# Two float32r products of a rounded sum and its difference in place of one fp32 product, for twelve means of squares

## The chip, the core and the metric

The kernel runs on one core of one Trainium2 chip. The metric is the device time of one execution in microseconds (us), the median over runs. Its engines work side by side, each through its own list of instructions in order, and wait for each other at semaphores: PE (TensorE, matrix products), ACT (ScalarE), DVE (VectorE), POOL (GpSimd) and SP (SyncE, which here issues the DMAs).

## The reference

A trunk of four layers over x of shape 1 x 512 x 1024. Each layer adds a token mixer and then a feed-forward layer to the residual stream, and each of the two starts with a root-mean-square norm:

```python
def _rmsnorm(x, g):
    xf = x.astype(jnp.float32)
    y = xf * lax.rsqrt(jnp.mean(xf * xf, axis=-1, keepdims=True) + EPS)
    return (y * g.astype(jnp.float32)).astype(x.dtype)

def _conv_ffn(h, w_up, conv_w, conv_b, w_down):
    u = _causal_dwconv(h @ w_up, conv_w, conv_b)
    return (jax.nn.silu(u[..., D_FF:]) * u[..., :D_FF]) @ w_down

for i in range(DEPTH):
    hn = _rmsnorm(x, mix_norm[i])
    ...
    x = x + mix.astype(x.dtype)
    x = x + _conv_ffn(_rmsnorm(x, ffn_norm[i]), ffn_w_up[i], ffn_conv_w[i], ffn_conv_b[i],
                      ffn_w_down[i]).astype(x.dtype)
```

The mixers are an RG-LRU block, a Mamba-2 SSD, sliding-window attention and HGRN2, in this order. HGRN2 has 8 heads, and normalises the output `o` of each head by itself, over its 128 features:

```python
    o = _rmsnorm(o, norm_w).reshape(bsz, s, D_MODEL) * jax.nn.silu(g_out.astype(jnp.float32))
```

## The kernel before

Everything is stored with features on the 128 partitions and the 512 tokens along the free dimension. x is 8 tiles of 128 x 512 (`k.x`). Weights come in panels of 128 x 1024 words by DMA into a ring of 4 (`k.w`). ACT rounds a panel to float32r (`round_until`, L250, into `w_big`), and POOL subtracts that from the panel and writes the difference as bf16 (`weights_gpsimd`, L266, four pieces of 128 x 256, into `w_rest`). A tile of a product with weights is then 8 float32r products (`in_big`, L295) and 8 bf16 products (`in_rest`, L305), summed in one PSUM bank; output products do the same at L337 and L341. POOL passes the panels strictly in order, in one loop over all panels at the end of the program.

A norm over features is a product with a constant 128 x 128 matrix `mean` of 1/1024: it sums over partitions and leaves the mean in every row. The squares are made by ACT (`square_x`, L399) and summed over the 8 tiles by DVE (`sum_squares`, L475, the last into `sqsum`). `norm_tensor` (L585) is the product, in fp32. ACT then takes the logarithm and the exponential (`inverse_root`, L553 and L556) for `rstd`, by which DVE scales what the projection left in PSUM (L693 in the feed-forward layer). The projection itself doesn't wait for the norm. In the feed-forward layer (`ffn_tensor`) `norm_tensor` stands inside panel 1, between its float32r and its bf16 products. ACT rounds panels 4 and 5 only after its first work on panels 0 and 1 (`ffn_scalar`), which needs `rstd`.

In the HGRN2 mixer `hgrn_events` writes out the order of all engines by hand. A slot holds half a panel of the projection ("half": 4 products L295, 4 products L305), one of 8 levels of the attention of an earlier head (L1833 to L1848, with DVE's updates L2018, L2019, L2021 and L2032 between two levels), and the steps of a "tail" of a still earlier head. A head takes 8 slots and 4 panels. Tail step 3 is the output of the head (L1879, L1882) and ACT's square of it (L1929, into `k.sq`); step 4, one slot later, is the mean (L1887, an fp32 product) and ACT's logarithm and exponential into `inner_factor`; steps 6 to 8 finish the head: DVE L2053, L2058, ACT L1937, DVE L2061, and after the last head PE needs L2061's output for the last products of the output projection (L337, L341). For the last two heads the slots have no projection left, and pieces of the output projection ("early") take its place.

## Time and profile before

| | |
|---|---|
| time, median of 3 runs | 1772.92 us (1772.85 to 1773.04) |
| the profiled execution's own time | 1772.94 us |
| its span in the trace | 1771.1 us |
| PE busy | 1720.5 us, 97% of the span |
| DVE, ACT, POOL busy | 1150.9, 1129.3, 1227.8 us |
| granted TensorE clock | 9 tenths or more in all 40 slices |

The span runs from the first instruction of the trace to the end of the last; 1.8 us of the execution's time lie outside it. Busy time of an engine counts a stretch in which several of its instructions overlap once. A record of a matrix product starts when it is issued and ends when its last column is out, so records in a row overlap, and it is the distance of two starts that says what a product costs. PEld is the loading of the weights of a product, which lies beside the products before it.

### The profile page before, as it was taken

Reading aid. Unit: us, or ns where it says so; the run is one execution under the profiler, and the core shown is the slowest. Engines: PE = TensorE matmul, PEld = TensorE weight load, DVE = VectorE, ACT = ScalarE, POOL = GpSimd, SP = SyncE. Lnnn points to the kernel's source line nnn. Section 1 sums busy time; section 2 is a strip of 40 time slices with the busy share of each in tenths; the row PEclk is TensorE's granted clock in tenths of the full one; section 3 lists DMA queues with packets and bytes.
Section 4 is the critical chain, followed back from the end, with each engine's and each line's share of the span. In section 5 each row is a group of like instructions: output and inputs, shape, how many; then the busy total and the mean of one; then the engine's idle time right before and its main releaser. Section 6 shows DMA issues by size and latency. Waiting matters only on the chain.

```text
span 1771.1 us, 27487 instructions
## 1 busy us (share of the span) xinstructions
PE 1720.5 (97%) x9861; PEld 1040.6 (59%) x10032; DVE 1150.9 (65%) x1873; ACT 1129.3 (64%) x1581; POOL 1227.8 (69%) x1788
## 2 busy tenths in 40 slices
PE   7989999999999999999999999999999999999999
PEld 4546666655555556666665666666655565566665
DVE  6886777228888754777226857776248877577720
ACT  8887666455977757666555877665454555866642
POOL 7747777877555647777877657778865554677785
PEclk9999999999999999999999999999999999999999
DMA  7323444545223225444543114444532222344453
GB/s 270 107 96 120 152 145 148 154 154 158 74 95 104 86 82 175 147 144 149 153 149 108 37 38 150 152 143 147 154 128 97 97 96 73 108 154 145 152 153 122
DMA packets 65615, 226.59 MB, mean 128 GB/s; under 512 B 8149, under 2 KB 9173, under 8 KB 64981
## 3 DMA queue, kind: packets, MB, share of 16 engines
q1 hardware_dynamic: 64236, 221.88, 39.6%
q10 hardware_dynamic: 1245, 2.95, 0.5%
q8 instruction: 80, 1.31, 0.3%
q14 instruction: 54, 0.44, 0.1%
HBM read 222.51 MB, written 2.10 MB: 127 GB/s over the span
## 4 chain that ended last, share of the span: by engine, by line
PE 73%; DVE 10%; ACT 8%; issue 5%; POOL 3%; DMA 1%; ACTq 0%; DVEq 0%; POOLq 0%
PE psum L295 22%; PE psum L305 21%; PE psum L337 12%; PE psum L341 11%; POOL w_rest L266 2%; ACT w_big L250 2%; DMA y_rest<-in_ssd_tables 1%; DVE psum L1621 1%; PE psum L1833 1%; PE psum L2241 1%; ACT psum L1468 1%; PE psum L2276 1%; DVE psum L1706 1%; PE psum L2258 1%; ACT L1501 1%
## 5 line engine op out<-in xcount | busy, mean ns | idle before, releaser
L266 POOL TENSOR_TENSOR w_rest<-w_panel,w_big 128x256 bf16<-128x256 f32 x1660 | 1163.9, 740 | 461.1 <-ACT w_big L250 461.1
L295 PE MATMUL psum<-x_big,w_big 128*128 128x512 f32 x2248 | 656.1, 425 | 8.5 <-ACT x_big L387 6.4
L305 PE MATMUL psum<-x_rest,w_rest 128*128 128x512 bf16 x2131 | 537.7, 382 | 8.7 <-DVE x_rest L483 1.7
L250 ACT ACTIVATE w_big<-w_panel 128x1024 fp32r<-128x1024 f32 (+1 forms) x415 | 418.4, 1032 | 171.9 <-PE psum L341 91.4
L295 PEld LDWEIGHTS psum<-x_big,w_big 128*128 128x128 f32 x2248 | 416.3, 189 | 134.7 <-issue 25.8
L305 PEld LDWEIGHTS psum<-x_rest,w_rest 128*128 128x128 bf16 x2248 | 188.6, 98 | 283.2 <-issue 102.6
L701 DVE SCALAR_TENSOR_TENSOR psum<-ffn_raw,params,psum 128x512 f32<-128x512 f32 x352 | 264.6, 752 | 7.2 <-ACT psum L655 1.0
L693 DVE TENSOR_TENSOR ffn_raw<-psum,rstd 128x512 f32<-128x512 f32 x176 | 121.4, 691 | 138.9 <-PE psum L305 120.3
L655 ACT ACTIVATE psum<-ffn_raw,params 128x512 f32<-128x512 f32 x176 | 137.4, 782 | 102.1 <-DVE ffn_raw L693 101.8
L337 PE MATMUL psum<-g_big,w_big 128*128 128x512 f32 x704 | 199.4, 423 | 0.0
L547 DVE SCALAR_TENSOR_TENSOR x_resid<-psum,x_resid 128x512 f32<-128x512 f32 x64 | 43.8, 689 | 225.0 <-PE psum L341 202.2
L341 PE MATMUL psum<-g_rest,w_rest 128*128 128x512 bf16 x677 | 165.4, 381 | 1.3
L337 PEld LDWEIGHTS psum<-g_big,w_big 128*128 128x128 f32 x704 | 133.2, 189 | 36.0
L662 ACT ACTIVATE g_big<-psum 128x512 fp32r<-128x512 f32 x88 | 52.5, 597 | 111.2 <-DVE psum L710 111.1
L341 PEld LDWEIGHTS psum<-g_rest,w_rest 128*128 128x128 bf16 x704 | 61.1, 98 | 87.8 <-issue 26.5
L337 PE MATMUL psum<-y_big,w_big 128*128 128x512 f32 x320 | 107.8, 459 | 2.1 <-DVE y_rest L2061 1.1
L483 DVE SCALAR_TENSOR_TENSOR x_rest<-x_big,psum 128x512 bf16<-128x512 f32 x64 | 43.9, 686 | 90.7 <-ACT psum L391 90.7
L341 PE MATMUL psum<-y_rest,w_rest 128*128 128x512 bf16 x298 | 84.1, 383 | 2.5 <-POOL w_rest L266 1.8
L337 PEld LDWEIGHTS psum<-y_big,w_big 128*128 128x128 f32 x320 | 60.3, 191 | 18.8 <-issue 5.2
L710 DVE TENSOR_TENSOR psum<-psum,ffn_silu_out 128x512 f32<-128x512 f32 x88 | 61.5, 699 | 7.0 <-ACT ffn_silu_out L678 4.1
L387 ACT ACTIVATE x_big<-x_resid,shifted_gain 128x512 fp32r<-128x512 f32 x64 | 45.4, 710 | 31.6 <-DVE x_resid L547 31.6
L714 DVE SCALAR_TENSOR_TENSOR g_rest<-g_big,psum 128x512 bf16<-128x512 f32 x88 | 59.8, 680 | 2.7 <-ACT g_big L662 2.7
(263 smaller groups left out, 1714.1 us busy)
## 6 DMA issues: line engine op xcount, KB each, us to landing
w_panel<-in_up SPq DMA_DIRECT2D x176, 512.0 KB, 3.5
w_panel<-in_dn SPq DMA_DIRECT2D x64, 448.0 KB, 3.3
w_panel<-in_ssd_in SPq DMA_DIRECT2D x41, 512.0 KB, 3.2
w_panel<-in_dn SPq DMA_DIRECT2D x32, 512.0 KB, 3.5
w_panel<-in_hgrn_in SPq DMA_DIRECT2D x32, 512.0 KB, 3.2
w_panel<-in_lru_in SPq DMA_DIRECT2D x18, 512.0 KB, 3.5
w_panel<-in_ssd_out SPq DMA_DIRECT2D x16, 512.0 KB, 3.2
w_panel<-in_swa_in SPq DMA_DIRECT2D x12, 512.0 KB, 3.2
```

What stands on the lines that cost most here:

```text
L250: act.activation(k.w1[:, slot, 0:words], k.w[:, slot, 0:words], ACT.Copy, scale=(SHIFT - 1) / SHIFT).then_inc(k.s("panel_big"), 1)
L266: rest = pool.tensor_tensor(k.w2[:, slot, a], k.w[:, slot, a], k.w1[:, slot, a].bitcast(F32), ALU.subtract)
L295: pe.matmul(out, k.w1[:, slot, q * m:(q + 1) * m], k.x1[:, q, :], start=q == 0, stop=False)
L305: mm = pe.matmul(out, k.w2[:, slot, q * m:(q + 1) * m], k.x2[:, q, :], start=False, stop=q == DT - 1)
L337: pe.matmul(out, k.w1[:, slot, (q - p0) * P:(q - p0 + 1) * P], y1[:, q, :], start=q == 0, stop=False)
L341: mm = pe.matmul(out, k.w2[:, slot, (q - p0) * P:(q - p0 + 1) * P], y2[:, q, :], start=False, stop=q == kt - 1)
L655: act.activation(out, k.ffn_raw[:, j % 2, half, 2:], ACT.Identity, bias=k.p("ffn_conv_b", j + (l * 2 * FF_T + half * FF_T)), scale=k.p("ff ...
L662: act.activation(k.g1[:, j, :], k.ps[:, lin_bank(j), :], ACT.Copy, scale=1 / SHIFT).then_inc(k.s("ffn_hi"), 1)
L693: dve.tensor_tensor(k.ffn_raw[:, j % 2, half, 2:], k.ps[:, k.bank(job, i), :], k.rstd[:, :], ALU.mult).then_inc(k.s("banks_free"), 1)
L701: dve.scalar_tensor_tensor(out, k.ffn_raw[:, j % 2, half, tap:tap + S], k.p("ffn_conv_w", j + ((l * 3 + tap) * 2 * FF_T + half * FF_T)), o ...
L710: dve.tensor_tensor(out, out, k.ffn_silu[:, j % 2, :], ALU.mult).then_inc(k.s("ffn_gated"), 1)
L714: dve.scalar_tensor_tensor(k.g2[:, j, :], k.g1[:, j, :].bitcast(F32), 1 - SHIFT, k.ps[:, lin_bank(j), :], ALU.mult, ALU.add).then_inc(k.s( ...
```

## The change

Twelve of the mean products change: the four of the feed-forward layers and the eight of HGRN2's heads. The other norms keep theirs. Instead of one fp32 product of `mean` with the squares there are two products in float32r: one with the squares rounded to float32r, one with what the rounding left, also float32r, added in the same PSUM bank.

In the feed-forward layer DVE makes the two parts from `sqsum` (`part_squares`: a copy that rounds, and a subtraction), and PE's two products move behind the bf16 products of panel 1 (`norm_in_parts`). In HGRN2 ACT squares the head's output twice, once in fp32 and once rounded (`x_sq_high`), and POOL subtracts (`hgrn_gpsimd`), at a place in its loop over the panels: before the weights of panel 4h + 11 for head h, and before panel 36 for the last. PE has the product with the rounded part first and the one with the rest behind it, each with its own wait. `mean` is rounded once to float32r at the start, by DVE. The new tiles lie over `x_sq` and `x_sqsum`; `mean_big` is new (512 bytes of each partition). The last piece is a semaphore: the SSD mixer's `ssd_ea` is now counted in `ssd_decays`.

```diff
+        self.sq_parts = sb("x_sq_parts", [P, 2, S], F32R)
+        self.sq_high = sb("x_sq_high", [P, S], F32R)
...
+        self.mean = sb("mean_big", [P, P], F32R)
...
+def part_squares(dve, k, c):
+
+    dve.wait_ge(k.s("sq_summed"), (DT - 1) * (c + 1))
+    dve.tensor_copy(k.sq_parts[:, 0, :], k.sqsum[:, :]).then_inc(k.s("sq_parted"), 1)
+    dve.wait_ge(k.s("sq_parted"), c + (HG_H if c == 2 * DEPTH - 1 else 0))
+    dve.tensor_tensor(k.sq_parts[:, 1, :], k.sqsum[:, :], k.sq_parts[:, 0, :].bitcast(F32), ALU.subtract
+                      ).then_inc(k.s("sq_parted"), 1)
...
             dve.wait_ge(k.s("params_landed"), 32)
+            dve.tensor_copy(k.mean[:, :], k.c("mean"))
             shift_gain(dve, k, 2, DEPTH - 1)
...
+        if c % 2:
+            part_squares(dve, k, c)
...
+def norm_in_parts(pe, k, l):
+
+    parted = 2 * l + (HG_H if l == DEPTH - 1 else 0)
+    pe.wait_ge(k.s("sq_parted"), parted + 1)
+    pe.matmul(k.ps[:, 4, :], k.mean[:, :], k.sq_parts[:, 0, :], start=True, stop=False)
+    pe.wait_ge(k.s("sq_parted"), parted + 2)
+    pe.matmul(k.ps[:, 4, :], k.mean[:, :], k.sq_parts[:, 1, :], start=False, stop=True
               ).then_inc(k.s("norm_summed"), 1)
...
-        if i == 1:
-            norm_tensor(pe, k, 2 * l + 1)
         pe.wait_ge(k.s("panel_split"), k.split(job, i))
         in_rest(pe, k, job, i, fresh=None if i else 2 * l + 1)
+        if i == 1:
+            norm_in_parts(pe, k, l)
...
-            pe.wait_ge(k.s("hgrn_sq"), h + 1)
-            pe.matmul(k.ps[:, 4, :], k.c("mean"), k.sq[:, h % 2, :], start=True, stop=True
+            pe.wait_ge(k.s("hgrn_sq"), 2 * h + 2)
+            pe.matmul(k.ps[:, 4, :], k.mean[:, :], k.sq_high[:, :], start=True, stop=False)
+            pe.wait_ge(k.s("sq_parted"), 2 * DEPTH - 2 + h + 1)
+            pe.matmul(k.ps[:, 4, :], k.mean[:, :], k.sq_parts[:, h % 2, :], start=False, stop=True
                       ).then_inc(k.s("hgrn_sum"), 1)
...
-            act.activation(k.sq[:, h % 2, :], k.ps[:, 7, :], ACT.Square, scale=mean_scale(P)).then_inc(k.s("hgrn_sq"), 1)
+            if h:
+                act.wait_ge(k.s("hgrn_sum"), h)
+            for out in (k.sq[:, h % 2, :], k.sq_high[:, :]):
+                act.activation(out, k.ps[:, 7, :], ACT.Square, scale=mean_scale(P)).then_inc(k.s("hgrn_sq"), 1)
...
+def hgrn_gpsimd(pool, k, panel):
+
+    for h in range(HG_H):
+        if panel == min(4 * h + 11, 4 * HG_H + 4):
+            pool.wait_ge(k.s("hgrn_sq"), 2 * h + 2)
+            sq = k.sq[:, h % 2, :]
+            pool.tensor_tensor(k.sq_parts[:, h % 2, :], sq, k.sq_high[:, :].bitcast(F32), ALU.subtract
+                               ).then_inc(k.s("sq_parted"), 1)
...
             for n in range(FIRST, len(PANELS)):
                 ssd_gpsimd(pool, k, n - k.panel0["ssd_in"])
+                hgrn_gpsimd(pool, k, n - k.panel0["hgrn_in"])
                 weights_gpsimd(pool, k, n)
```

Three places of the order of instructions, of before and then of the change. The numbers of lines are those of each kernel: L295, L305, L1833, L1887 and L266 of before are L301, L311, L1861, L1915 with L1917, and L272 of the change. First PE, around the mean of one head in HGRN2, before:

```order
L295 MATMUL psum<-x_big,w_big 128x512 x4
L305 MATMUL psum<-x_rest,w_rest 128x512 [waits panel_split]
L305 MATMUL psum<-x_rest,w_rest 128x512 x3
L1833 MATMUL psum<-arena 32x16 [waits hgrn_attn,hgrn_update]
L1833 MATMUL psum<-arena 32x16 x15
L1887 MATMUL psum<-x_sq,consts 128x512 [waits hgrn_sq]
L295 MATMUL psum<-x_big,w_big 128x512 [waits banks_free,panel_big]
```

The same place of the change:

```order
L301 MATMUL psum<-x_big,w_big 128x512 x4
L311 MATMUL psum<-x_rest,w_rest 128x512 [waits panel_split]
L311 MATMUL psum<-x_rest,w_rest 128x512 x3
L1861 MATMUL psum<-arena 32x16 [waits hgrn_attn,hgrn_update]
L1861 MATMUL psum<-arena 32x16 x15
L1915 MATMUL psum<-x_sq_high,mean_big 128x512 [waits hgrn_sq]
L1917 MATMUL psum<-x_sq_parts,mean_big 128x512 [waits sq_parted]
L301 MATMUL psum<-x_big,w_big 128x512 [waits banks_free,panel_big]
```

Nothing moved; the second product has a wait of its own, on POOL, and the next half of a panel stands behind it. Next POOL in the change, the stretch that has the subtractions of the last two heads (of before it is L266 throughout):

```order
L272 TENSOR_TENSOR w_rest<-w_panel,w_big 128x256 [waits panel_big]
L272 TENSOR_TENSOR w_rest<-w_panel,w_big 128x256 x3
L1984 TENSOR_TENSOR x_sq_parts<-x_sq,x_sq_high 128x512 [waits hgrn_sq]
L272 TENSOR_TENSOR w_rest<-w_panel,w_big 128x256 [waits panel_big]
L272 TENSOR_TENSOR w_rest<-w_panel,w_big 128x256 x3
L1984 TENSOR_TENSOR x_sq_parts<-x_sq,x_sq_high 128x512 [waits hgrn_sq]
L272 TENSOR_TENSOR w_rest<-w_panel,w_big 128x256 [waits panel_big]
```

For each head the subtraction stands behind the four pieces of panel 4h + 10 and ahead of those of panel 4h + 11; that of the last head follows the panel behind its predecessor's. Last PE in a feed-forward layer, panel 1, before:

```order
L295 MATMUL psum<-x_big,w_big 128x512 x7
L585 MATMUL psum<-x_sqsum,consts 128x512 [waits sq_summed]
L305 MATMUL psum<-x_rest,w_rest 128x512 [waits panel_split]
L305 MATMUL psum<-x_rest,w_rest 128x512 x7
L295 MATMUL psum<-x_big,w_big 128x512 [waits banks_free,panel_big]
```

The same place of the change:

```order
L301 MATMUL psum<-x_big,w_big 128x512 x7
L311 MATMUL psum<-x_rest,w_rest 128x512 [waits panel_split]
L311 MATMUL psum<-x_rest,w_rest 128x512 x7
L611 MATMUL psum<-x_sq_parts,mean_big 128x512 [waits sq_parted]
L613 MATMUL psum<-x_sq_parts,mean_big 128x512 [waits sq_parted]
L301 MATMUL psum<-x_big,w_big 128x512 [waits banks_free,panel_big]
```

The mean moved behind the 8 bf16 products of panel 1.

## Rows read from the trace of the kernel before

**Rows 1.** The page: its chain of waits by engine; PE's busy time.

```profile
PE 73%; DVE 10%; ACT 8%; issue 5%; POOL 3%; DMA 1%; ACTq 0%; DVEq 0%; POOLq 0%
...
PE 1720.5 (97%) x9861; PEld 1040.6 (59%) x10032; DVE 1150.9 (65%) x1873; ACT 1129.3 (64%) x1581; POOL 1227.8 (69%) x1788
```

**Rows 2.** Stretch of one HGRN2 head: length, busy us (count) by engine, clock, DMA.

```profile
1394.59:1417.85 23.26, 22.83 (x316) 14.06 (x319) 18.81 (x43) 12.51 (x16) 12.06 (x17) 1.00 0.29 92
```

**Rows 3.** Timeline, PE, last feed-forward layer: start, length, engine, line, tiles, count, idle before.

```profile
1531.60 0.50 PE L295 MATMUL psum<-x_big,w_big 128*128 128x512 f32 x1 [0.18 <-ACT x_big L387]
1531.94 1.90 PE L305 MATMUL psum<-x_rest,w_rest 128*128 128x512 bf16 x8
1533.49 2.21 PE L295 MATMUL psum<-x_big,w_big 128*128 128x512 f32 x8
1535.54 1.02 PE L585 MATMUL psum<-x_sqsum,consts 128*128 128x512 f32 x2
...
1537.94 2.17 PE L295 MATMUL psum<-x_big,w_big 128*128 128x512 f32 x8
1539.95 1.90 PE L305 MATMUL psum<-x_rest,w_rest 128*128 128x512 bf16 x8
1541.50 2.19 PE L295 MATMUL psum<-x_big,w_big 128*128 128x512 f32 x8
...
1547.11 1.25 PE L305 MATMUL psum<-x_rest,w_rest 128*128 128x512 bf16 x5
```

**Rows 4.** Timeline of the same stretch, DVE, ACT and POOL.

```profile
1533.63 0.69 DVE L475 TENSOR_TENSOR x_sqsum<-x_sq,psum 128x512 f32<-128x512 f32 x1
1536.60 0.69 ACT L553 ACTIVATE rstd<-psum,params 128x512 f32<-128x512 f32 x1 [0.20 <-PE psum L585]
1542.59 2.81 POOL L266 TENSOR_TENSOR w_rest<-w_panel,w_big 128x256 bf16<-128x256 f32 x4 [2.79 <-ACT w_big L250]
```

**Rows 5.** Timeline, one HGRN2 head (the third): ACT, PE, POOL, DVE.

```profile
1395.78 0.60 ACT L1929 ACTIVATE x_sq<-psum 128x512 f32<-128x512 f32 x1 [0.32 <-PE psum L1882]
1397.86 1.13 PE L1887 MATMUL psum<-x_sq,consts 128*128 128x512 f32 x2
1394.59 2.80 POOL L266 TENSOR_TENSOR w_rest<-w_panel,w_big 128x256 bf16<-128x256 f32 x4 [6.82 <-ACT w_big L250]
1398.73 1.01 DVE L2019 TENSOR_TENSOR arena<-arena 128x256 f32<-128x256 f32 x1
1401.54 0.41 DVE L2019 TENSOR_TENSOR arena<-arena 128x256 f32<-128x256 f32 x1
```

**Rows 6.** Timeline in the SSD mixer: POOL on 128 x 512, and PE behind it.

```profile
474.15 1.28 POOL L1548 TENSOR_TENSOR x_sqsum<-x_sqsum,x_sq 128x512 f32<-128x512 f32 x1 [1.83 <-ACT x_sq L1508]
475.48 0.30 PEld L1380 LDWEIGHTS psum<-x_sqsum,consts 128*128 128x128 f32 x2 [0.62 <-POOL x_sqsum L1548]
```

**Rows 7.** Timeline, HGRN2, seventh head: POOL and PE.

```profile
1487.64 2.79 POOL L266 TENSOR_TENSOR w_rest<-w_panel,w_big 128x256 bf16<-128x256 f32 x4 [6.84 <-ACT w_big L250]
1490.01 1.13 PE L1887 MATMUL psum<-x_sq,consts 128*128 128x512 f32 x2
1492.32 0.45 PE L1833 MATMUL psum<-arena 128*32 128x16 f32 x32 [0.28 <-DVE arena L2021]
```

**Rows 8.** Timeline, HGRN2, last head: ACT, then PE in the output projection.

```profile
1504.07 0.60 ACT L1929 ACTIVATE x_sq<-psum 128x512 f32<-128x512 f32 x1 [4.00 <-PE psum L1882]
1505.98 0.69 ACT L553 ACTIVATE inner_factor<-psum,params 128x512 f32<-128x512 f32 x1
1511.54 0.50 PE L337 MATMUL psum<-y_big,w_big 128*128 128x512 f32 x1 [1.11 <-DVE y_rest L2061]
```

**Rows 9.** Timeline, PE near the program's start.

```profile
19.87 0.60 PE L305 MATMUL psum<-x_rest,w_rest 128*128 128x512 bf16 x2 [0.78 <-DVE x_rest L483]
```

**Rows 10.** Groups by line and shape: copies of DVE and POOL; busy us, mean ns.

```profile
L1695 DVE COPY x_sqsum<-x_sq 128x512 f32<-128x512 f32 x1 | 0.4, 417 | 0.0
L1546 POOL COPY x_sqsum<-x_sq 128x512 f32<-128x512 f32 x3 | 1.8, 610 | 10.9 <-ACT x_sq L1508 10.9
```

More of the change, by code:

```diff
@@ L150, in __init__ @@
         self.factor = sb("inner_factor", [P, S])
+        at = self._at
         self.sq = sb("x_sq", [P, 2, S])
         self.sqsum = sb("x_sqsum", [P, S])
+        after, self._at = self._at, at
+        self.sq_parts = sb("x_sq_parts", [P, 2, S], F32R)
+        self.sq_high = sb("x_sq_high", [P, S], F32R)
+        self._at = after
         self.par = sb("params", [P, NPARAM])
@@ L585, in norm_tensor @@
     pe.matmul(k.ps[:, 4, :], k.c("mean"), k.sqsum[:, :], start=True, stop=True
+              ).then_inc(k.s("norm_summed"), 1)
+def norm_in_parts(pe, k, l):
[4 more added lines that the diff above has]
+    pe.matmul(k.ps[:, 4, :], k.mean[:, :], k.sq_parts[:, 1, :], start=False, stop=True
               ).then_inc(k.s("norm_summed"), 1)
@@ L1293, in turn @@
             if g == 0:
-                pe.wait_ge(k.s("ssd_decays"), 2)
+                pe.wait_ge(k.s("ssd_decays"), 3)
                 pe.wait_ge(k.s("ssd_dt_t"), 3)
@@ L1449, in dt @@
             return
-        act.activation(b.ea, k.p("ssd_a_log"), ACT.Exp).then_inc(k.s("ssd_ea"), 1)
+        act.activation(b.ea, k.p("ssd_a_log"), ACT.Exp).then_inc(k.s("ssd_decays"), 1)
         act.wait_ge(k.s("banks_free"), k.evicted("ssd_in", 0))
@@ L1576, in dt @@
             softplus_join(dve, softplus, b.size, b.q, b.dt)
-            dve.wait_ge(k.s("ssd_ea"), 1)
+            dve.wait_ge(k.s("ssd_decays"), 1)
             dve.wait_ge(k.s("ssd_ones"), 16)
@@ L1588, in decays @@
         if part == 2:
-            dve.wait_ge(k.s("ssd_decays"), 2)
+            dve.wait_ge(k.s("ssd_decays"), 3)
             dve.tensor_tensor(b.dt_end.rearrange("p c h -> p (c h)"), k.ps[:, 5, P:2 * P],
```

## The prediction

> **What bounds the kernel now.** I read the page first, then the stretches of HGRN2 and the timelines around the twelve products. The chain that ended last is PE for 73% and PE is busy for 97% of the span [rows 1]. In the middle of HGRN2 a head takes 23.26 us, of which PE is busy 22.83, while DVE has 18.81, ACT 12.51 and POOL 12.06 [rows 2]; the clock is 1.00, the 2.4 GHz level, throughout. So a product less on PE is time won, and a wait of PE is time lost at once, since its list is in order. What is left to ask at each of the twelve places is whether both parts are there when PE comes.
>
> **The product itself.** In the feed-forward layer panel 1, with the mean inside, runs from 1533.49 to 1537.94, 4.45 us; panel 2, without it, from 1537.94 to 1541.50, 3.56 [rows 3]. The fp32 product costs 0.89 us. It stands in the trace as two records (x2). Sixteen products in 3.56 us are 0.22 each; the float32r half alone, 8 from 1537.94 to 1539.95, gives 0.25 at most. I take 0.235 for one float32r product, 0.47 for the pair: 0.42 less on PE where nothing waits, bounds 0.39 and 0.45.
>
> The Trainium skill (Perfetto Trace Analysis, Engine Utilization) halves TensorE's output rate for what it calls FP32_LOW_HIGH. Taken for a whole fp32 product that would be 0.43 us, as much as the new pair, and the sum would lose its whole gain; the row has 0.89 for it, so here the halving holds for each of the two records. The measurement decides.
>
> **Feed-forward layers, four times.** DVE's last sum ends at 1533.63 + 0.69 = 1534.32 [rows 4]. The rounding copy is 0.42 as the nearest row [rows 10], the subtraction has the shape of L475, 0.69: both are done by 1535.5, or about 1536.5 if POOL, which works at this time, holds each up by half a microsecond. PE comes to the pair only after panel 1's bf16 products, at 1533.49 + 3.56 = 1537.05. No wait there. Cost of these two on DVE: nothing, DVE waits for `rstd` afterwards.
>
> But the norm is later. The second product starts at 1537.28 and lasts 0.4 (2.17 us for eight that start 0.25 apart [rows 3]), so the pair ends at about 1537.7 where the fp32 product ended at 1536.56 (1535.54 + 1.02), so ACT's logarithm moves from 1536.60 [rows 4] to about 1537.75, by 1.15 us, and with it the scaling, ACT's rounding of panels 4 and 5, and POOL's differences. POOL finishes panel 4 at 1542.59 + 2.81 = 1545.40; that becomes 1546.55, and 1546.60 at PE. PE wants panel 4's bf16 products at 1547.11 [rows 3] less 0.42 = 1546.69. It fits by 0.1 us; I charge nothing, with 0.2 each as the upper bound. Term: 4 x -0.42 = -1.7 (bounds -1.8 and -0.9).
>
> **HGRN2, heads 0 to 5.** The place is the same in all six, as in [rows 5]. ACT's square ends at 1396.38; the second one, again 0.60, at about 1397.0. PE comes to the first product at 1397.86: no wait. POOL is the question. It starts on panel 4h + 10 at 1394.59 and ends its four pieces at 1397.39; the subtraction stands behind them. POOL on two fp32 inputs of 128 x 512 takes 1.28 us, and PE's weight load starts 0.05 us behind it (475.43 to 475.48) [rows 6]. So the rest is there at 1397.39 + 1.28 + 0.05 = 1398.72, 0.86 us after PE came, and 0.6 after it has finished the first product. Behind a wait a float32r product takes 0.34 until the next one starts (1531.60 to 1531.94) [rows 3], since its weights aren't loaded ahead. PE goes on at 1399.06; before it was 1397.86 + 0.89 = 1398.75. A head costs 0.31 us more instead of 0.42 less: 6 x 0.31 = +1.9. What is queued behind the waiting product is the next half of a panel, then the next level of the attention, for which DVE waits; there it is all later by the same 0.3. POOL's next panel is 1.28 later, but PE needs it three panels on. Bounds: a POOL instruction of that shape cannot be much under the copy, 0.61 [rows 10], which would give no wait (1398.05) and -0.42 a head; and if DVE keeps it off by half a microsecond, as each holds the other up below, +0.8 a head.
>
> That they do hold each other up is in [rows 5]: DVE's L2019 on 128 x 256 takes 1.01 us at 1398.73, while POOL runs, and 0.41 at 1401.54, when POOL has stopped. The subtraction starts in a stretch in which DVE is idle, so I take the undisturbed 1.28.
>
> The Trainium skill (SBUF — State Buffer, Who interferes with whom) says that a DVE instruction with two SBUF inputs and a GpSimd instruction that reads SBUF exclude each other for a whole instruction, and whichever starts first wins. By the rows just named it holds here. It speaks against this change, as POOL's work in HGRN2 grows by 1.28 us a head, and is the second rival below.
>
> **Head 6.** Here the slots are shorter. POOL is done with its four pieces at 1487.64 + 2.79 = 1490.43 [rows 7], the rest reaches PE at 1490.43 + 1.28 + 0.05 = 1491.76, PE goes on at 1492.10 instead of 1490.01 + 0.89 = 1490.90: +1.2. Before, PE then waited for DVE until 1492.32 with 0.28 idle, which gives some of it back; but POOL's panel 35 now also runs 1.28 later into DVE's next level, which takes some again. Term: +1.1, bounds 0.7 and 1.6.
>
> **Head 7.** POOL is free, and the chain is short of everything: in the output projection PE waits 1.11 us for this head's L2061 at 1511.54 [rows 8]. So each added step counts in full. The square ends at 1504.67; the second square adds 0.60 (1505.27), POOL 0.05 + 1.28 (1506.60), PE's second product starts at 1506.65 and ends 0.50 later (the record at 1531.60 [rows 3]), and with the same small distance the logarithm starts at about 1507.2 instead of 1505.98: +1.25, bounds 1.1 and 1.6. PE's filler in between gets 1.4 later and still ends before.
>
> **The start.** DVE's copy of `mean` stands ahead of a sum and of an `x_rest` for which PE waits for 0.78 us [rows 9]. A copy of 128 x 512 takes 0.42 [rows 10], a quarter of it with the fixed part perhaps 0.15: +0.15 (0 to 0.3).
>
> **Nothing else.** The semaphore renamed in the SSD mixer is waited for at the same places. ACT's eight squares in heads 0 to 6 and POOL's 1.28 us a head lie on engines half idle [rows 2]. No DMA is moved.
>
> **Sum**, against the profiled execution's own time of 1772.94: -1.7 + 1.9 + 1.1 + 1.25 + 0.15 = +2.7, so 1775.6; the median of the runs shown is 0.02 lower, which changes nothing. With every term at its lower bound it would be -1.8 - 2.5 + 0.7 + 1.1 + 0 = -2.5 (1770.4), with every term at its upper -0.9 + 4.8 + 1.6 + 1.6 + 0.3 = +7.4 (1780.3); all at once is unlikely at either end. A measurement of this kernel can tell 0.2%, 3.5 us, from no change: below 1769.4 is faster, above 1776.4 slower. The forecast is within, on the slow side.
>
> **The rivals.**
> 1. *PE waits for POOL* (the forecast): 1775.6. Chance 0.53.
> 2. *POOL and DVE hold each other up* (slower). POOL's subtraction and the panel behind it fall into DVE's updates of the next levels; DVE's L2021 ends later than PE comes to the level, in each of the six heads, or DVE holds the subtraction itself up. If it is 0.5 us a head for six heads and 0.4 in the last two: +2.7 + 3.4 = +6.1, 1779. For it: L2019's 1.01 us. Against it: DVE idles long before this place and PE's own delay gives it 0.3 us. It decides if more than about 0.3 us of DVE's delay isn't covered by PE's. Chance 0.2.
> 3. *Both parts are there in time* (the other side). All twelve pairs save 0.42: -5.0 + 0.15, 1768.1, faster. It needs the rest at PE by 1398.1, a subtraction in under 0.7 us or POOL starting earlier. For it: POOL's copy of that size takes 0.61. Against: L1548 with the same operands takes 1.28, and even at 0.65 the last head's chain has grown by the second square and the subtraction. Chance 0.1.
> 4. *The pair costs what the fp32 product did*, that is the change doesn't do what it says: the feed-forward term is 0 and HGRN2's heads get the second product's half more, 8 x 0.2: +2.7 + 1.7 + 1.6 = +6.0, 1778.9. Against: 0.25 at most for a float32r product in rows 3. Chance 0.05.
> The remaining 0.12 is for what I don't see, spread to both sides.
>
> **How the numbers follow.** Predicted is the first case, 1775.6. The range is 1771.0 to 1779.0: its lower end leaves out rival 3 and half of the unseen, its upper end takes in most of rival 2. Slower: rivals 2 and 4 (0.24), a fifth of the forecast whose terms are all near their upper bounds (0.11), and part of the unseen: 0.38. Faster: rival 3 and a little: 0.12. Within 0.2%: 0.50.
>
> **What would show it.** In the profile after: PE's second product of heads 0 to 5 waits about 0.6 us for POOL's L1984, which starts when its four pieces end and takes 1.28; a head takes 23.57 us instead of 23.26; the last head's `inner_factor` starts 3.1 us after the start of the first square instead of 1.9; in the feed-forward layers the second product ends 1.1 us later in its panel than the fp32 one and PE doesn't wait at panel 4. It is wrong if L1984 takes well under or over 1.28, if PE waits at DVE's L2021 more than before, or if PE's gain in the feed-forward layers isn't 0.42 each.

## The result, and the profile after

The change takes 1775.55 us (median of 20 runs, 1774.9 to 1776.6) where the kernel before takes 1772.84 (20 runs beside them, 1772.2 to 1773.15): +2.7 us, ratio 1.0016, 95% interval 1.0009 to 1.0023. That is slower, by less than the 0.2% that the prediction called no change. The profiled execution spans 1773.6 us (before 1771.1). Of all executions in this document two are left out of every median and comparison, one of the kernel before (9918 us) and one of experiment 7 (2470 us, at a granted clock of 0.655).

The page, its chain by engine and its busy times, which answer to [rows 1]:

```profile
PE 1718.4 (97%) x9861; PEld 1039.2 (59%) x10032; DVE 1164.5 (66%) x1882; ACT 1132.5 (64%) x1589; POOL 1242.3 (70%) x1796
...
PE 72%; DVE 10%; ACT 8%; issue 5%; POOL 4%; DMA 1%; ACTq 0%; DVEq 0%; POOLq 0%
```

PE works 2.1 us less and the span is 2.5 us longer, so PE waits 4.6 us more. The waits of PE that are new or have grown most, from the list of waits (us in total, times, longest):

```profile
PE psum L1917 <- POOL x_sq_parts L1984: 4.0, 8, 1.2
...
PE psum L1915 <- ACT x_sq_high L1962: 1.2, 1, 1.2
```

The first is the wait of the second product of each of the eight heads for POOL's subtraction. The second is the last head's wait for the second square, where the kernel before waited 0.7 us for its one square; 4.0 and 0.5 are nearly all of the 4.6.

**Heads 0 to 5.** The stretch of one head, with the same columns as [rows 2]:

```profile
1393.94:1417.48 23.54, 22.78 (x315) 14.06 (x319) 19.57 (x43) 12.90 (x17) 13.64 (x17) 1.00 0.28 91
```

A head takes 23.54 us instead of 23.26, PE is busy 0.05 less, DVE 0.76 more in the same 43 instructions, POOL 1.58 more. From one head's square to the next it is 23.52 to 23.55 in all six. The third head in the timeline, as [rows 5] before:

```profile
1397.26 0.50 PE L1915 MATMUL psum<-x_sq_high,mean_big 128*128 128x512 f32 x1
1398.09 0.50 PE L1917 MATMUL psum<-x_sq_parts,mean_big 128*128 128x512 f32 x1 [0.32 <-POOL x_sq_parts L1984]
1398.42 1.09 PE L301 MATMUL psum<-x_big,w_big 128*128 128x512 f32 x4
1399.36 1.04 PE L311 MATMUL psum<-x_rest,w_rest 128*128 128x512 bf16 x4
1400.32 0.45 PE L1861 MATMUL psum<-arena 128*32 128x16 f32 x32
...
1405.18 0.64 PE L1876 MATMUL psum<-arena 128*32 128x64 f32 x16
...
1395.19 0.60 ACT L1962 ACTIVATE x_sq<-psum 128x512 f32<-128x512 f32 x1 [0.32 <-PE psum L1910]
1395.68 0.59 ACT L1962 ACTIVATE x_sq_high<-psum 128x512 fp32r<-128x512 f32 x1
...
1393.99 2.80 POOL L272 TENSOR_TENSOR w_rest<-w_panel,w_big 128x256 bf16<-128x256 f32 x4 [6.85 <-ACT w_big L256]
1396.76 1.27 POOL L1984 TENSOR_TENSOR x_sq_parts<-x_sq,x_sq_high 128x512 fp32r<-128x512 f32 x1
1397.99 3.17 POOL L272 TENSOR_TENSOR w_rest<-w_panel,w_big 128x256 bf16<-128x256 f32 x4
1402.50 3.21 POOL L272 TENSOR_TENSOR w_rest<-w_panel,w_big 128x256 bf16<-128x256 f32 x4 [1.34 <-ACT w_big L256]
...
1398.93 0.95 DVE L2064 TENSOR_TENSOR arena<-arena 128x256 f32<-128x256 f32 x1
...
1403.28 0.97 DVE L2062 TENSOR_TENSOR arena<-arena 128x256 f32<-128x256 f32 x1
1404.18 0.94 DVE L2064 TENSOR_TENSOR arena<-arena 128x256 f32<-128x256 f32 x1
```

POOL's L1984 stands right behind its four pieces, takes 1.27 us and ends at 1398.03; PE's second product starts at 1398.09 and the half panel behind it 0.33 later. That is the wait that was forecast. Two details matter below. DVE's L2064 (L2021 of before) ends at 1399.88, and the next level, which needs it, starts at 1400.32, so PE's own delay leaves DVE 0.44 us here. Two levels later L2064 ends at 1405.12 and PE's L1876 starts at 1405.18: there PE comes no sooner than DVE lets it.

**The last two heads.** PE, ACT, with [rows 7, 8] for before:

```profile
1492.22 0.50 PE L1917 MATMUL psum<-x_sq_parts,mean_big 128*128 128x512 f32 x1 [1.20 <-POOL x_sq_parts L1984]
...
1508.15 0.50 PE L1917 MATMUL psum<-x_sq_parts,mean_big 128*128 128x512 f32 x1 [0.85 <-POOL x_sq_parts L1984]
...
1514.24 0.50 PE L343 MATMUL psum<-y_big,w_big 128*128 128x512 f32 x1 [1.00 <-DVE y_rest L2104]
...
1505.67 0.60 ACT L1962 ACTIVATE x_sq<-psum 128x512 f32<-128x512 f32 x1 [4.00 <-PE psum L1910]
...
1508.68 0.69 ACT L571 ACTIVATE inner_factor<-psum,params 128x512 f32<-128x512 f32 x1 [0.63 <-PE psum L1917]
```

From the seventh head's square to the last one's it is 16.33 us instead of 15.24 (+1.09). In the last head `inner_factor` starts 3.01 us after the square instead of 1.91 (+1.10).

**The feed-forward layers.** The last one, PE, ACT and DVE, as [rows 3, 4] before:

```profile
1536.19 2.19 PE L301 MATMUL psum<-x_big,w_big 128*128 128x512 f32 x8
...
1539.78 0.58 PE L611 MATMUL psum<-x_sq_parts,mean_big 128*128 128x512 f32 x1
1540.20 0.39 PE L613 MATMUL psum<-x_sq_parts,mean_big 128*128 128x512 f32 x1
1540.43 2.02 PE L301 MATMUL psum<-x_big,w_big 128*128 128x512 f32 x8
...
1547.43 2.19 PE L301 MATMUL psum<-x_big,w_big 128*128 128x512 f32 x8
...
1551.06 2.20 PE L301 MATMUL psum<-x_big,w_big 128*128 128x512 f32 x8
...
1540.63 0.69 ACT L571 ACTIVATE rstd<-psum,params 128x512 f32<-128x512 f32 x1 [1.53 <-PE psum L613]
...
1536.33 0.69 DVE L481 TENSOR_TENSOR x_sqsum<-x_sq,psum 128x512 f32<-128x512 f32 x1
1537.05 0.90 DVE L488 CAST x_sq_parts<-x_sqsum 128x512 fp32r<-128x512 f32 x1
1537.98 1.11 DVE L490 TENSOR_TENSOR x_sq_parts<-x_sqsum,x_sq_parts 128x512 fp32r<-128x512 f32 x1
```

PE waits for neither part. Panel 1 with the pair takes 4.24 us (1536.19 to 1540.43) instead of 4.45, and the panel behind it gives back another 0.17. From the first weight load of panel 1 to that of panel 3 it is 7.61 to 7.66 us in the four layers, before 8.00 to 8.04: -0.40 each. Then the panel with tile 4 takes 3.63 instead of 3.58, and a few hundredths follow; at panel 8 the layers stand at -0.28 to -0.31, so 0.1 us each is given back.

### The profile page after: what moved, and what is told of

Its sections match the earlier page's. It is cut to its first block, busy times and chain, and to the rows that moved or that the text cites. A ratio compares the mean times of both kernels' runs of the same rounds, so it can differ in the third digit from the quotient of the medians.

```text
span 1773.6 us, 27519 instructions
## 1 busy us (share of the span) xinstructions
PE 1718.4 (97%) x9861; PEld 1039.2 (59%) x10032; DVE 1164.5 (66%) x1882; ACT 1132.5 (64%) x1589; POOL 1242.3 (70%) x1796
## 4 chain that ended last, share of the span: by engine, by line
PE 72%; DVE 10%; ACT 8%; issue 5%; POOL 4%; DMA 1%; ACTq 0%; DVEq 0%; POOLq 0%
PE psum L301 22%; PE psum L311 21%; PE psum L343 12%; PE psum L347 11%; POOL w_rest L272 3%; ACT w_big L256 2%; DMA y_rest<-in_ssd_tables 1%; DVE psum L1649 1%; PE psum L2284 1%; ACT psum L1496 1%; PE psum L1861 1%; PE psum L2319 1%; DVE psum L1734 1%; POOL x_sq_parts L1984 1%; PE psum L2301 1%
## 5 line engine op out<-in xcount | busy, mean ns | idle before, releaser
L272 POOL TENSOR_TENSOR w_rest<-w_panel,w_big 128x256 bf16<-128x256 f32 x1660 | 1168.8, 742 | 437.8 <-ACT w_big L256 437.8
L301 PE MATMUL psum<-x_big,w_big 128*128 128x512 f32 x2248 | 652.3, 423 | 8.7 <-ACT x_big L393 6.6
L311 PE MATMUL psum<-x_rest,w_rest 128*128 128x512 bf16 x2131 | 537.1, 381 | 8.8 <-DVE x_rest L498 1.9
L301 PEld LDWEIGHTS psum<-x_big,w_big 128*128 128x128 f32 x2248 | 415.7, 189 | 132.8 <-issue 23.6
L311 PEld LDWEIGHTS psum<-x_rest,w_rest 128*128 128x128 bf16 x2248 | 188.3, 98 | 282.0 <-issue 101.1
```

The lines of the kernel that those rows point to most:

```text
L272: rest = pool.tensor_tensor(k.w2[:, slot, a], k.w[:, slot, a], k.w1[:, slot, a].bitcast(F32), ALU.subtract)
L301: pe.matmul(out, k.w1[:, slot, q * m:(q + 1) * m], k.x1[:, q, :], start=q == 0, stop=False)
L311: mm = pe.matmul(out, k.w2[:, slot, q * m:(q + 1) * m], k.x2[:, q, :], start=False, stop=q == DT - 1)
```

## The experiments

Times in one table, each beside the kernel before on the same chip (1772.84 for the change, 1772.93 to 1772.99 for the experiments). "Head" is the distance between the squares of two neighbouring heads among the first seven, in the profiled execution. An interval that holds 1, as in 1, 8 and 11, doesn't tell the time from that of the kernel before by itself; what these three are used for is read from their traces. The eleven executions of 1 (1771.13 to 1772.34 us) and the 28 of the kernel before beside them (1772.34 to 1773.72) meet only at their ends all the same.

| | us | ratio to before, 95% | head |
|---|---|---|---|
| before | 1772.9 | | 23.26 |
| the change | 1775.55 | 1.0009 to 1.0023 | 23.53 |
| 1: feed-forward part alone | 1771.76 | 0.9985 to 1.0002 | 23.25 |
| 2: HGRN2 part alone | 1777.35 | 1.0016 to 1.0035 | 23.54 |
| 3: subtraction one panel earlier | 1777.74 | 1.0016 to 1.0036 | 23.5 to 23.6 |
| 4: PE's pair one slot later | 1776.19 | 1.0011 to 1.0028 | 23.58 |
| 5: one product, nothing subtracted | 1771.33 | 0.9981 to 0.9998 | 22.62 |
| 6: DVE subtracts | 1771.09 | 0.9981 to 0.9999 | 22.88 to 22.99 |
| 7: as 5, POOL has less to do | 1768.58 | 0.9965 to 0.9984 | 22.62 |
| 8: as 1, pair inside panel 1 | 1771.72 | 0.9985 to 1.0002 | 23.26 |
| 9: as 6, last head in fp32 | 1770.53 | 0.9978 to 0.9995 | 22.88 to 22.97 |
| 10: the change, POOL has less to do | 1775.30 | 1.0003 to 1.0022 | 23.43 |
| 11: 4 and 10 together | 1772.95 | 0.9991 to 1.0009 | 23.02 |

**1 and 2, the two halves of the change.** In 1 HGRN2's squares, product and place in POOL's loop are those of before, in 2 `norm_tensor` of the feed-forward layers is.

```diff
-                hgrn_gpsimd(pool, k, n - k.panel0["hgrn_in"])
```

> HGRN2's heads go back to the fp32 product without POOL's subtraction and ACT's second square; the feed-forward layers keep the pair. Theory (PE saves 0.4 us per pair where the parts are ready, and loses in HGRN2 by waiting for POOL): 0.15 us more at the start, 0.3 less in each feed-forward layer, so 1 us below the kernel before, about 1771.8. Rival (the pair is no cheaper than one fp32 product, all of the change's difference is in products): same as before or up to 0.9 us (a third of the change's +2.7) above it.

```diff
-        if c % 2:
-            part_squares(dve, k, c)
...
-        if i == 1:
-            norm_in_parts(pe, k, l)
+        if i == 1:
+            norm_tensor(pe, k, 2 * l + 1)
```

> The feed-forward layers go back to the fp32 product in its old place; HGRN2 keeps the pair, POOL's subtraction and the second square. Theory: 0.15 at the start, 6 heads x 0.27, head 6 1.1 and head 7 1.1 more: +3.95, about 1776.8, slower than the change as a whole. Rival (the loss is spread over all twelve places): about +1.8, 1774.6.

Measured 1771.76 and 1777.35: -1.2 and +4.4, together +3.2 where the change has +2.7. Both halves do what their terms say, the first as a gain, the second as a loss. Heads take 23.25 us in 1, as before, and 23.54 in 2, as in the change. In the profile of 2 the first head's square is already 0.6 us late (1349.84 against 1349.27 before), though nothing but the copy of `mean` is added ahead of it; in the change it is 1.1 early, of which three feed-forward layers make 0.9. What stands ahead of HGRN2 varies by some tenths from trace to trace, and that is as much as the 0.5 by which the halves don't add up.

**3, the subtraction one panel earlier in POOL's loop**, ahead of panel 4h + 10 instead of 4h + 11, so that it is done before PE comes.

```diff
-        if panel == min(4 * h + 11, 4 * HG_H + 4):
+        if panel == min(4 * h + 10, 4 * HG_H + 4):
```

> POOL's subtraction of heads 0 to 6 stands one panel earlier, before panel 4h+10. Theory: in heads 0 to 5 POOL waits for the second square and subtracts at once, PE's wait falls from about 0.6 to 0.1 us, a head costs 0.3 less than before instead of 0.25 more: -1.8 for six heads; heads 6 and 7 as in the change (+2.2), feed-forward -1.2, start +0.15: -0.65, about 1772.2. Rival (POOL and DVE hold each other up, it is the added POOL work that costs): POOL's two panels end 3 us later and fall wholly into DVE's updates of the next levels, so no gain or a loss against the change: 1775.5 or more.

Measured 1777.74: the theory that PE's wait is the whole matter failed. In heads 0 to 5 PE's second product doesn't wait for POOL any more (in head 6 it still does, for 0.81 us), yet those heads keep their 23.5 to 23.6 us. In the third head the level behind the pair starts 4.72 us after the square, 0.22 sooner than before the change, and the head still ends 0.28 later than then, so the loss lies behind that slot. POOL now waits for the head's square before it may touch panel 4h + 10, and then works without a pause beside DVE's updates. Its timeline, and the wait of PE that grew, from the list of waits (in the change that row has 2.3 us):

```profile
1349.81 1.27 POOL L1984 TENSOR_TENSOR x_sq_parts<-x_sq,x_sq_high 128x512 fp32r<-128x512 f32 x1 [9.71 <-ACT x_sq_high L1962]
1351.04 13.67 POOL L272 TENSOR_TENSOR w_rest<-w_panel,w_big 128x256 bf16<-128x256 f32 x16
```

```profile
PE psum L1907 <- DVE arena L2091: 4.9, 8, 1.5
```

More than half of what 3 has above the change comes behind the seventh head: from its square to the last one's it is 17.59 us instead of 16.33. There POOL works on two panels for 6.59 us without a pause, and PE waits for DVE's L2064 before three levels, 0.43, 0.97 and 0.92 us.

**4, PE's pair one slot later** in heads 0 to 6, behind the next level and 2.3 us after L1984 is done.

```diff
-        elif t == 4:
+        elif t == (4 if h == HG_H - 1 else 5):
```

> PE's pair of heads 0 to 6 stands one slot later (about 2.8 us of PE's other work later); POOL, ACT and DVE do what they do in the change. Theory (it is PE's wait that costs): no wait at POOL's L1984 in heads 0 to 6, each of heads 0 to 5 costs 0.4 less than before, head 6 about nothing, head 7 still +1.1, feed-forward -1.2, start +0.15: -2.4, about 1770.4. Rival (contention of POOL with DVE costs, and PE would wait for DVE's updates anyway): the heads keep their 23.5 us, about 1775.5.

Measured 1776.19, heads 23.58: no gain, and the theory failed again, as in 3. The third head:

```profile
1399.64 0.44 PE L1861 MATMUL psum<-arena 128*32 128x16 f32 x32 [0.59 <-DVE arena L2064]
1400.01 0.50 PE L1915 MATMUL psum<-x_sq_high,mean_big 128*128 128x512 f32 x1
1400.35 0.39 PE L1917 MATMUL psum<-x_sq_parts,mean_big 128*128 128x512 f32 x1
...
1398.64 0.94 DVE L2064 TENSOR_TENSOR arena<-arena 128x256 f32<-128x256 f32 x1
```

The pair no longer waits, and in its place the level waits for DVE's L2064, which ran beside POOL and took 0.94. PE then still has the pair before it, 0.56 us (1400.01 to 1400.57). The profiled execution of 4 took as long as the change's (1775.56 and 1775.45 us). Its median is 0.6 higher, and part of that is the clock: its executions at a mean granted clock of 1.000 took 1775.63 to 1776.12 us, those at 0.999 up to 1777.11, and the profiled one has the granted clock at 0.50 for some 3.3 us in the last head.

**5 and 7, one product of the rounded squares.** 5 leaves out the second square, POOL's subtraction and the second product, so the mean is that of the rounded squares; 7 also leaves out three of POOL's four pieces of panels 4h + 11, so that part of the weights' differences isn't computed.

```diff
-            for out in (k.sq[:, h % 2, :], k.sq_high[:, :]):
-                act.activation(out, k.ps[:, 7, :], ACT.Square, scale=mean_scale(P)).then_inc(k.s("hgrn_sq"), 1)
+            act.activation(k.sq_high[:, :], k.ps[:, 7, :], ACT.Square, scale=mean_scale(P)).then_inc(k.s("hgrn_sq"), 1)
...
-                hgrn_gpsimd(pool, k, n - k.panel0["hgrn_in"])
```

> HGRN2's heads have one float32r product alone, of the rounded squares (the rest that the rounding leaves is left out of the mean), no subtraction on POOL and no second square; the feed-forward layers keep the pair (alone 1771.8). PE's product is 0.65 us shorter than the fp32 one and nothing is waited for. Theory of the prediction (in heads 0 to 5 PE's own work is the bound): 8 x -0.65 = -5.2, about 1766.6. Theory after the last runs (in the slot of the mean the next level waits for DVE's three updates, which POOL's panel holds up by 1.5 us, and the fp32 product only fills that time): a head gains 0.1 to 0.2 us, the last 0.4: about 1770.6.

```diff
+    short = 11 <= at_hgrn < 4 * HG_H and at_hgrn % 4 == 3
-    for at in range(0, words, PIECE):
+    for at in range(3 * PIECE if short else 0, words, PIECE):
```

> As e5_one_product, and POOL leaves out three of the four pieces of each panel 4h+11 of HGRN2's input (those products use what the ring held before), so that it isn't at work during DVE's updates in the slot of the mean. Theory of the prediction: as e5 without it, 1766.6, whatever POOL does. Theory after the last runs: DVE's L2062 and L2064 fall from 1.0 and 0.95 to 0.41 there, the level no longer waits, and the whole 0.65 a head comes: 3 us or more below e5, about 1767.

Measured 1771.33 and 1768.58. Both profiles show heads of 22.62, 0.64 less than before. But the profiled execution of 5 took 1768.39 us, and the other ten took 1770.56 to 1771.98, so that its profile is not that of a typical run; 7 has no such gap (1767.49 profiled, the others 1768.1 to 1769.3). With less for POOL to do, the median falls by 2.75 us. Where the typical run of 5 loses them isn't on record: no trace of one was taken. Two of DVE's updates in the slot of the mean, beside POOL in 5, and the second of them alone in 7:

```profile
1396.24 0.19 DVE L2058 TENSOR_TENSOR arena<-arena 128x32 f32<-128x32 f32 x1 [2.93 <-PE psum L1861]
...
1397.24 0.95 DVE L2061 TENSOR_TENSOR arena<-arena 128x256 f32<-128x256 f32 x1
```

```profile
1395.83 0.42 DVE L2063 TENSOR_TENSOR arena<-arena 128x256 f32<-128x256 f32 x1
```

The profiled execution of 5 shows one thing more. The small update L2058, the first of the slot, took 0.19 us there; at the same place it took 0.67 in the change and 0.80 before. So DVE was done 4.17 us after the square, where in the change it was 4.69, and PE, which came at 4.31, didn't wait. With the 0.67 of the change DVE would be done at about 4.65 and each head be some 0.35 us longer, which in seven heads is 2.4 us, near the 2.9 between this execution and the median of 5. That is an estimate from these rows, and no trace of a typical execution shows it.

**10 and 11, whether PE's wait costs anything.** Experiments 3 and 4 took PE's wait away and gained nothing. Either that wait is harmless, or each of the two put something in its place. 10 is the change with POOL's three pieces left out, 11 has the later pair of 4 as well; that part of the weights' differences isn't computed in either.

```diff
+    short = 11 <= at_hgrn < 4 * HG_H and at_hgrn % 4 == 3
-    for at in range(0, words, PIECE):
+    for at in range(3 * PIECE if short else 0, words, PIECE):
```

> The change itself, but POOL leaves out three of the four pieces of panels 4h + 11, the ones behind its subtraction; that part of the weights' differences is not computed. POOL is then away from DVE's updates of the next levels (PE's wait for the subtraction stays as it is). Theory 'two limits' (PE's wait for POOL and DVE's updates beside POOL are each enough to keep a head near 23.5): heads 0 to 5 take 23.3 to 23.5 us, the time is 1774 to 1775.5 us. Rival 'DVE's updates alone': heads at 22.9, 1771 us.

```diff
-        elif t == 4:
+        elif t == (4 if h == HG_H - 1 else 5):
```

> Both limits taken away at once: PE's pair one slot later in heads 0 to 6, and POOL leaves out three of the four pieces of panels 4h + 11; that part of the weights' differences is not computed. Theory 'two limits': heads 0 to 5 fall to 22.85 us (0.41 under the kernel before), the time is 1770.5 us (1769.5 to 1771.5), where each of the two alone stays at 1774 or more. Rival (something third holds the heads at 23.5): 1775 us or more.

| length of a head, us | POOL as in the change | POOL has less to do |
|---|---|---|
| pair in its place | 23.53 | 23.43 |
| pair one slot later | 23.58 | 23.02 |

With the pair in its place POOL's work matters little (0.10); with the pair one slot later it decides (0.56). The third head's rows show why: the level behind the pair, and DVE's update that it needs. 10, then 11:

```profile
1398.65 0.50 PE L1919 MATMUL psum<-x_sq_parts,mean_big 128*128 128x512 f32 x1 [0.33 <-POOL x_sq_parts L1986]
...
1400.88 0.30 PE L1863 MATMUL psum<-arena 128*32 128x16 f32 x13
...
1399.50 0.41 DVE L2066 TENSOR_TENSOR arena<-arena 128x256 f32<-128x256 f32 x1
```

```profile
1398.51 0.45 PE L1863 MATMUL psum<-arena 128*32 128x16 f32 x32
...
1398.05 0.41 DVE L2066 TENSOR_TENSOR arena<-arena 128x256 f32<-128x256 f32 x1
```

In 10 DVE is done at 1399.91, and PE, held by the subtraction, comes 0.97 later. In 11 DVE is done at 1398.46 and PE starts at 1398.51. The same for all kernels of interest, counted from the start of the third head's (first) square, to about 0.01 us:

| us after the square | DVE's update done | level starts | pair, or fp32 product | next level starts |
|---|---|---|---|---|
| before | 4.82 | 4.94 | ahead | 7.32 |
| the change | 4.69 | 5.13 | ahead, with a wait | 7.52 |
| 4 | 4.68 | 4.73 | behind | 7.57 |
| 10 | 4.17 | 5.13 | ahead, with a wait | 7.51 |
| 11 | 4.16 | 4.21 | behind | 7.05 |
| 6 | 4.61 | 4.66 | ahead, no wait | 7.06 |
| 5, as profiled | 4.17 | 4.31 | ahead, one product | 6.68 |

Beside POOL, DVE's update is a floor for the level: the level can't start before it. It lies at 4.6 to 4.8 in the four rows in which POOL is beside all of DVE's updates (before, the change, 4 and 6) and at 4.2 in 10 and 11; only the profiled execution of 5 has 4.2 with POOL there. What PE does ahead of the level costs nothing up to there. In the change the wait lifts PE over the floor, by 0.44. In 4 PE reaches the floor early, idles, and then pays the pair behind it in full: the wait is gone and so is the cover. In 11 the floor itself is 0.5 lower. So PE's wait is the cause in its slot, and moving the pair was no cure.

Of 11's time the 1770.5 that was expected failed, by 2.4. The six heads took 23.02 instead of 22.85, which is 1.0 us. In the seventh the level now waits 1.67 us for DVE, in 4 and in 11 alike, in place of the change's wait for POOL; so 4 has 16.31 us from the seventh square to the last, no less than the change's 16.33, where "about nothing" above the 15.24 of before was expected. In 11 that stretch is even 17.22, and there it is the clock. PE in 11 behind the wait, and the stretch from that level to the start of L1890, which follows two levels later; then the same stretch in 4, from 1493.22 to L1888 (the columns are those of [rows 2]):

```profile
1490.40 0.45 PE L1863 MATMUL psum<-arena 128*32 128x16 f32 x32 [1.67 <-DVE arena L2066]
...
1490.40:1496.89 6.49, 6.49 (x78) 3.64 (x79) 4.66 (x13) 2.60 (x3) 2.18 (x3) 0.74 0.35 126
```

```profile
1493.22:1498.80 5.58, 5.08 (x79) 2.92 (x79) 4.68 (x13) 2.60 (x3) 2.18 (x3) 1.00 0.33 106
```

The granted clock was at 1.00 during the wait, fell to its lower level of 1.2 GHz about 0.7 us behind it and was back at about 1494.3 (mean 0.51 between). That made the stretch 0.91 us longer than in 4, where the clock stayed at 1.00 behind the same wait; why it fell in one and not in the other is open. Eight of 11's ten executions have a mean granted clock of 0.999 and took 1772.74 to 1773.90 us, the two at 1.000 took 1772.04 and 1772.34. For the profiled executions, 6 x 0.51 less and 0.9 more is -2.2 against the change; their times differ by 2.1 (1773.36 and 1775.45).

**6 and 9, DVE subtracts.** DVE idles when the second square is done. In 6 it takes the subtraction from POOL in all eight heads; in 9 the last head goes back to one square and the fp32 product, since its chain has nothing to hide the pair's steps. 9 contains the edit of 6.

```diff
-                hgrn_gpsimd(pool, k, n - k.panel0["hgrn_in"])
...
+        if t == 3:
+            dve.wait_ge(k.s("hgrn_sq"), 2 * h + 2)
+            dve.tensor_tensor(k.sq_parts[:, h % 2, :], k.sq[:, h % 2, :], k.sq_high[:, :].bitcast(F32), ALU.subtract
+                              ).then_inc(k.s("sq_parted"), 1)
```

> The change with its subtraction in HGRN2 on DVE, in the 2.9 us in which DVE idles before the slot of the mean, and nothing of it on POOL; the pair, both squares and the feed-forward layers as in the change. Theory (POOL's extra 1.28 us delays PE's second product and pushes POOL's panel further over DVE's updates): heads 0 to 5 are at or up to 0.2 us below their 23.26 before, head 6 about as before, head 7 +0.6 (second square, 0.69 for 1.28): 1771.8 with the feed-forward layers' gain, 3.8 below the change. Rival (any second product and second square costs what the change does): 1775.5.

```diff
+            if h == HG_H - 1:
+                pe.wait_ge(k.s("hgrn_sq"), 2 * h + 1)
+                pe.matmul(k.ps[:, 4, :], k.c("mean"), k.sq[:, h % 2, :], start=True, stop=True
+                          ).then_inc(k.s("hgrn_sum"), 1)
+                return
```

> The version in which DVE subtracts, and the last head keeps the fp32 product with one square. The last head's chain then has no second square (0.49 us) and no subtraction (0.69) but an fp32 product for two float32r ones (0.42 more): 0.6 to 0.8 us less than with the pair. Theory: heads 0 to 5 stay at 22.9 us, the time is 1770.4 us against 1771.1 with the pair in all eight heads and 1772.9 before. Rival (the last head's chain is covered by PE's other work there): 1771.1 again.

Measured 1771.09 and 1770.53. Both beat the kernel before; 9 is the fastest version that computes everything, 2.4 us under before and 5.0 under the change. The third head in 6, DVE and PE:

```profile
1395.66 1.05 DVE L2086 TENSOR_TENSOR x_sq_parts<-x_sq,x_sq_high 128x512 fp32r<-128x512 f32 x1 [1.83 <-ACT x_sq_high L1962]
...
1398.20 0.94 DVE L2064 TENSOR_TENSOR arena<-arena 128x256 f32<-128x256 f32 x1
```

```profile
1396.62 0.50 PE L1915 MATMUL psum<-x_sq_high,mean_big 128*128 128x512 f32 x1
1396.96 0.39 PE L1917 MATMUL psum<-x_sq_parts,mean_big 128*128 128x512 f32 x1
...
1399.20 0.45 PE L1861 MATMUL psum<-arena 128*32 128x16 f32 x32
```

The rest is there at 1396.71, and both products run without a wait. The level starts at 1399.20, 0.06 behind the end of L2064 at 1399.14: PE is back at DVE's floor, and this head gains 0.27 us of the 0.40 that the pair saves on PE. Not every head has the floor there. In the fourth and fifth head of 6, and in four of the six heads of 9, DVE's first update of 128 x 256 took 0.41 instead of 1.00, DVE was done at 4.0 us behind the square instead of 4.6, the level started at 4.53 to 4.56 instead of 4.64 to 4.66, and the head took 22.88 to 22.90 us, where the others took 22.94 to 22.99. So the floor shows within one kernel, and what it takes from the pair is about 0.1 us a head. The last two heads still lose in 6: PE waits 0.54 and 0.23 us for the subtraction, from the seventh square to the last it is 15.89 us instead of 15.24, and `inner_factor` starts 2.40 us behind the last square instead of 1.91. In 9 that last distance is 1.91 again.

**8, the feed-forward pair inside panel 1**, three bf16 products earlier, so that `rstd` is sooner. It is built on experiment 1.

```diff
+        if i == 1:
+            in_rest(pe, k, job, i, 0, 5)
+            norm_in_parts(pe, k, l)
+            in_rest(pe, k, job, i, 5, DT)
```

> Feed-forward layers alone (HGRN2 as before), with the pair behind the fifth of panel 1's eight bf16 products instead of behind the eighth. In the changed kernel 0.1 us of each layer's 0.4 was lost again at panel 4, whose differences on POOL come too late because the norm is 1.1 us later. Theory: the norm is 0.65 us earlier, the 0.1 comes back, 4 x 0.1: 1771.4 against 1771.8. Rival (the 0.1 has another cause): 1771.8; or, if DVE's parts are late, a wait of PE of some tenths in each: 1772.2.

Measured 1771.72 against 1771.76: no difference that the times can tell. In the traces the panel with tile 4 takes 3.58 us again, as before the change, and the layers stand at -0.33 to -0.40 at panel 8, where experiment 1 has -0.28 to -0.33; 4 x 0.07 is 0.3 us and lies within the spread of the runs. So the trace bears out that the later norm costs at panel 4, and the time can't tell it.

## Why the prediction was right

The forecast was 1775.6 and the measurement 1775.55. The signs, the places and the wait were foreseen; that the sum fits to 0.05 us is luck, since a gain of the feed-forward layers that is 0.5 us smaller than forecast is made up by the heads, which lose 0.4 less, and by 0.3 in a place where nothing was forecast. The terms, as the two profiled executions show them:

| term | forecast | measured |
|---|---|---|
| start | +0.15 | +0.15 |
| feed-forward, 4 layers | -1.7 | -1.2 |
| heads 0 to 5 | +1.9 | +1.63 |
| head 6 | +1.1 | +1.09 |
| head 7 | +1.25 | +1.10 |
| "nothing else" | 0 | -0.3 |
| sum | +2.7 | +2.5 |

**The product.** -0.42 for a pair that waits for nothing: -0.40. Rival 4 is out.

**Feed-forward layers.** No wait at the pair, as forecast; DVE's parts took 0.90 and 1.11 us beside POOL, each within the half microsecond more that I had allowed for that, and ended (1539.09) before PE came (1539.78). The step that was mis-sized is "it fits by 0.1 us; I charge nothing". The logarithm came 1.33 us later in its panel (1540.63 - 1536.19 = 4.44 against 3.11 in [rows 3, 4]), not 1.15, because the pair's second product starts 0.42 behind the first, not 0.23. POOL's differences for tile 4 were then just late, and 0.1 us a layer went. It was inside the upper bound of 0.2.

**HGRN2, heads 0 to 5.** Mechanism and place were right: L1984 behind the four pieces, 1.27 us against 1.28, the second product 0.06 behind it. The forecast of 0.31 a head came out as 0.27, but it is made of two parts, of which I had one. PE's wait costs 0.2 in its slot: from the first product to the start of the half panel's bf16 products it is 2.10 us (1397.26 to 1399.36), where the fp32 product and the same four products took 1.90 before. The other 0.1 comes two levels later. There POOL's panel starts 7.31 us after the square instead of 7.45, and DVE's updates come 0.18 later than before. In this head L2062 and L2064 take 0.97 and 0.94, where in the kernel before only the second was long (0.41 and 0.95). L2064 ends at 1405.12, and PE comes no sooner. With POOL's three pieces left out, in experiment 10, both the long first update and this delay are gone, and a head is 0.10 shorter. That is rival 2's mechanism, DVE and POOL in each other's way, at a fifth of its price and at a later level than it named.

**What the forecast did not see** is DVE's floor under this slot. I had argued that "PE's own delay gives it 0.3 us", and in the change DVE's update is ready 0.44 us before PE comes. But then not all of PE's time here is worth saving: before the change the level started only 0.12 us behind DVE's update, at 4.94 against 4.82. So the pair's 0.42 couldn't all be had, nor can the pair be put one slot later for nothing, which my expectation for experiment 4 missed: 1770.4 was expected, 1776.2 came. In experiment 3 (1772.2 expected, 1777.7 measured) it was DVE's updates further on that took back what the slot had gained. It also lowers rival 3 somewhat. With both parts in time, in experiment 6, a head gains 0.27 to 0.32 with the floor at 4.6 and 0.36 to 0.38 with it at 4.0, and not 0.42. The -5.0 of that case also counts a saving in the last head, whose chain grows by the second square whatever POOL does.

**Head 6 and head 7.** +1.09 and +1.10. Head 6 went as in the working: counted from its square, PE goes on behind the pair 1.15 us later than behind the fp32 product before (forecast 1.2), the next level starts only 0.72 later, as PE's wait for DVE there is gone, and the level after it 1.09 later, as it waits 0.81 for DVE instead of 0.44. In the last head the second square started 0.49 us behind the first and not 0.60, which is most of the difference from the working; PE waits 1.00 us for the head's result where it waited 1.11.

**The rest.** The -0.3 lies in the SSD mixer, where PE waits for a DMA (1.3 us in the trace of before, 1.0 here, 1.7 in experiment 10 and 0.9 in 11). The instructions there are the same, so I take it as variation from execution to execution and claim no cause for it.

## What to carry to other kernels

A product saved on the busiest engine is worth its time only where its operands don't come later: four places gained 0.3 us each with operands made on an engine that had time, and eight lost 0.3 to 1.1 with one more step on the way. Before a wait is taken away by moving the work, look for the next thing that holds the same instruction: work ahead of such a floor is free, the same work behind it is paid in full. Give an added step to the engine that is idle at that moment, not to the one with the lowest share of the stretch: here POOL was busy for 12.06 us of a head and DVE for 18.81, and the step was cheaper on DVE.
